# Expert weights of a mixture layer moved as one transfer per expert on one Trainium2 core

## The reference, cut to what matters

```python
combine = jnp.sum(jax.nn.one_hot(expert_idx, N_EXPERTS, dtype=jnp.float32) * weights[..., None], axis=1)
for e in range(N_EXPERTS):
    h = jax.nn.silu(t @ w_gate[e]) * (t @ w_up[e])
    out = out + combine[:, e:e + 1] * (h @ w_down[e])
```

## Time and profile before

| | |
|---|---|
| Median of 3 runs | 1083.51 us (1080.67 to 1083.88) |
| The profiled execution, its time | 1081.82 us |
| Its span, from the first to the last instruction | 1080.1 us |
| Busy share of the span: PE matmul, PE weight load | 76%, 59% |
| Busy share: DVE, ACT, POOL | 29%, 18%, 1% |
| Mean granted PE clock, as a share of 2.4 GHz | 0.902 |
| Read from HBM, mean rate | 437.84 MB, 406 GB/s |
| Chain that ended last, by engine | DMA 61%, PE 34%, ACT 2% |
| Weight transfers of experts (gate, up, down into the ring) | 62, 62, 60 of 2048 KB |

### The profile page before, as it was taken

One profiled execution on the slowest core, in us unless ns is written; L12 is line 12 of the kernel. 1 busy time (PEld: TensorE's weight loads), 2 busy tenths in 40 slices (PEclk: granted clock), 3 DMA queues, 4 the chain that ended last, 5 costly groups with the idle time before them and its releaser, 6 DMA issues.

```text
span 1080.1 us, 30413 instructions
## 1 busy us (share of the span) xinstructions
PE 817.0 (76%) x13908; PEld 634.1 (59%) x13909; DVE 315.9 (29%) x783; ACT 193.4 (18%) x358; POOL 5.5 (1%) x26
## 2 busy tenths in 40 slices
PE   7999997665666767586799998967576766766864
PEld 7888665554454545464499986745354554544652
DVE  5764522111111111121277744311111111111212
ACT  6674211000000000010163330100000000000002
POOL 1000000000000000000000000000000000000000
PEclk9999899888898888988999999988889888798988
DMA  9977999999999999999998599999999999999996
GB/s 356 426 296 313 408 427 429 430 428 428 428 428 429 428 429 430 428 427 424 418 427 361 220 396 420 428 428 429 429 427 428 429 428 428 428 431 428 425 424 255
DMA packets 35872, 439.62 MB, mean 407 GB/s; under 512 B 4208, under 2 KB 4976, under 8 KB 9968
## 3 DMA queue, kind: packets, MB, share of 16 engines
q1 hardware_dynamic: 34848, 437.58, 96.3%
q10 hardware_dynamic: 976, 1.33, 0.4%
HBM read 437.84 MB, written 1.05 MB: 406 GB/s over the span
## 4 chain that ended last, share of the span: by engine, by line
DMA 61%; PE 34%; ACT 2%; issue 2%; DVE 1%; SPq 0%; ACTq 0%; DVEq 0%
DMA ring<-in_w_up 34%; DMA ring<-in_w_down 27%; PE psum L1295 8%; PE psum L1487 8%; PE psum L1360 4%; PE psum L1496 4%; PE psum L1504 2%; PE psum L1342 2%; PE psum L1516 2%; PE psum L1274 1%; PE psum L1568 1%; DMA ring<-in_even_first 1%; PE psum L1510 1%; ACT ring_halves L538 0%; PE psum L1267 0%
## 5 line engine op out<-in xcount | busy, mean ns | idle before, releaser
L1487 PE MATMUL psum<-ring,m 128*32 128x128 f32 x7936 | 309.7, 321 | 220.8 <-DMA ring<-in_w_gate 106.7
L1487 PEld LDWEIGHTS psum<-ring,m 128*32 128x32 f32 x7936 | 271.8, 130 | 266.2 <-issue 114.3
L1160 DVE TENSOR_TENSOR m<-psum,m 128x128 f32<-128x128 f32 x64 | 18.7, 292 | 568.5 <-ACT m L703 568.5
L1496 PE MATMUL psum<-ring,m 128*32 128x256 f32 x1984 | 121.1, 382 | 15.6 <-DMA ring<-in_w_down 11.5
L703 ACT ACTIVATE m<-psum 128x128 f32<-128x128 f32 x64 | 17.7, 277 | 519.1 <-PE psum L1487 519.1
L1295 PE MATMUL psum<-scr_halves,ring_halves 128*128 128x256 f32 x768 | 105.2, 284 | 5.1 <-DVE ring_halves L802 4.5
L1496 PEld LDWEIGHTS psum<-ring,m 128*32 128x32 f32 x1984 | 65.8, 111 | 64.3 <-issue 22.6
L1295 PEld LDWEIGHTS psum<-scr_halves,ring_halves 128*128 128x128 f32 x768 | 99.3, 192 | 5.7 <-DVE ring_halves L802 4.9
L1504 PE MATMUL psum<-m 32*128 32x256 f32 x1056 | 84.8, 427 | 8.0 <-issue 5.9
L802 DVE TENSOR_TENSOR ring_halves<-ring,ring_halves 128x2048 fp32r<-128x2048 f32 (+2 forms) x37 | 68.6, 1885 | 13.6 <-ACT ring_halves L538 13.5
L1516 PE MATMUL psum<-x,m 128*32 128x256 f32 x1024 | 71.1, 397 | 0.0
(11 more groups left out here) (192 smaller groups left out, 483.9 us busy)
## 6 DMA issues: line engine op xcount, KB each, us to landing
ring<-in_w_gate SPq DMA_DIRECT2D x62, 2048.0 KB, 40.5
ring<-in_w_up SPq DMA_DIRECT2D x62, 2048.0 KB, 40.6
ring<-in_w_down SPq DMA_DIRECT2D x60, 2048.0 KB, 41.1
ring<-in_odd_w_in SPq DMA_DIRECT2D x5, 2048.0 KB, 26.1
ring<-in_even_w_in SPq DMA_DIRECT2D x3, 2048.0 KB, 20.6
ring<-in_even_w_out SPq DMA_DIRECT2D x2, 2048.0 KB, 30.4
spare<-in_w_down SPq DMA_DIRECT2D x2, 2048.0 KB, 22.9
ring<-in_last_down SPq DMA_DIRECT2D x8, 512.0 KB, 36.7
```

Of the source, the lines that this page charges most:

```text
L1487: last = pe.matmul(GU[CAP * part:CAP * (part + 1), lo:lo + FP], block_of(k), w_of(k)[:, FP * part:FP * (part + 1)], start=k == 0, stop=k = ...
L1496: last = pe.matmul(YB[CAP * part:CAP * (part + 1), 0:DP], hhT[:, CAP * f:CAP * (f + 1)], w[:, f, DP * part:DP * (part + 1)], start=f == 0, ...
```

## The change

The weights of an expert are laid out by the host as one array, in which each partition's row holds gate, up and down behind each other (48 KB). What follows from that in the kernel:

- Experts 6 to 30 are loaded **whole**: one transfer of 128 rows of 48 KB into three slots side by side, after a wait for `y_ready` of the expert three before. Experts 0, 1, 3, 4, 5 and 31 keep single transfers of one matrix (16 KB rows), as does expert 2.
- EARLY is **expert 2** instead of 27: it lies in the mixers' buffers, and experts 0, 1 and 3 (RING_FIRST) are those that are in the ring first. The order of the first loads in layer 1 begins with the down matrix of expert 3.
- Slots are numbered from another start (`place`), and one entry of the ring (HOLE) is left empty between the odd mixer and layer 1, so that three slots of an expert lie side by side.
- The overflow part moves to the **middle** of the layer (after expert 14) on every engine, SP's part between the loads of expert 17 and 18. It uses another of the three token buffers.
- The loops: PE has experts 0 to 5 written out, then a loop of three experts for 6 to 14, the overflow part, a second loop of three for 15 to 29, and experts 30 and 31 written out. That is 14 bodies of `expert` per layer. DVE and ACT have two loops of three, and two written out.

```diff
-EARLY = TURNS * TRI
-DRAIN = EARLY + 1
+EARLY = 2
+RING_FIRST = (0, 1, 3)
+MIDDLE = 5
+PAUSE = MIDDLE * TRI - 1
+SPARE_XG = 1
...
+FINE = 2 * TRI
+ROLLED = FINE // TRI
...
+def is_whole(e):
+    return FINE <= e < NE - 1
...
             def first(l, i, mat):
-                n = L_MOE[l] + 3 * i + mat
-                fill(n, matrix(l, i, mat), buffer(n, mat))
-
-            def expert(l, b, i):
-                e = b * TRI + i
-                for mat, used in enumerate((gate_used, gu_ready, y_ready)):
-                    n = L_MOE[l] + 3 * i + mat
-                    sp.wait_ge(used, after(l, e - TRI))
-                    load(n, matrix(l, e, mat), buffer(n, mat))
...
+                n = entry(l, RING_FIRST[i]) + mat
+                fill(n, matrix(l, RING_FIRST[i], mat), buffer(n, mat))
+
+            def second(l, e):
+
+                for mat in range(3):
+                    n = entry(l, e) + mat
+                    fill(n, matrix(l, e, mat), buffer(n, mat))
+
+            def whole(l, e, i, former):
+
+                sp.wait_ge(y_ready, after(l, former))
+                at = third(l, (i - 1) % TRI) * 3 * SLOT
+                sp.dma_start(ring[:, at:at + 3 * SLOT], expert_weights_in[l, e]).then_inc(whole_landed[third(l, (i - 1) % TRI)], 16)
...
+                for e in range(EARLY + 2, FINE):
+                    second(l, e)
+                for i in range(TRI):
+                    e = FINE + i
+                    whole(l, e, i, e - TRI)
+                turns(l, ROLLED + 1, MIDDLE + 1)
+                overflow(l)
+                turns(l, MIDDLE + 1, TURNS)
...
-                with pe.Fori(0, TURNS) as T:
-                    for i in range(TRI):
-                        expert(l, T, i)
-                for e in range(EARLY, NE):
-                    expert(l, e // TRI, e % TRI, rest=True)
-                    if e == DRAIN:
-                        scatter_result(l, e)
+                for e in range(FINE):
+                    expert(l, e // TRI, e % TRI)
+                for start, stop in ((ROLLED, MIDDLE), (MIDDLE, TURNS)):
+                    with pe.Fori(start, stop) as T:
+                        for i in range(TRI):
+                            expert(l, T, i)
+                    if start == ROLLED:
                         more_experts(l)
+                for e in range(TURNS * TRI, NE):
+                    expert(l, e // TRI, e % TRI)
```

More of the change, by code:

```diff
@@ L38 @@
 TRI = 3
[L39 to L40 removed]
+TURNS = NE // TRI
 MAX_MORE = (S - 1) // CAP
@@ L59, with entry, place, third @@
 SPLIT = [L_EVEN + i for i in range(7)] + [L_ODD + i for i in range(8)]
+def entry(l, e):
+    return L_MOE[l] + 3 * (e - (e > EARLY))
+def place(n):
+    return (n + 2) % RING
+def third(l, i):
+    return place(L_MOE[l] + 3 * i) // 3
+def is_whole(e):
+    return FINE <= e < NE - 1
+SINGLE = [z for z in SPLIT if z not in (L_EVEN, L_EVEN + 1, L_ODD)]
+for layer in range(2):
+    for expert in range(FINE):
+        if expert != EARLY:
+            SINGLE += [entry(layer, expert) + mat for mat in range(3)]
+    SINGLE += [entry(layer, NE - 1) + mat for mat in range(2)]
+SINGLE.append(L_GAIN)
+WHOLE = [(layer, expert) for layer in range(2) for expert in range(NE) if is_whole(expert)]
+def single_count(n):
+    return sum(z <= n and place(z) == place(n) for z in SINGLE)
+def whole_count(l, e):
+    return sum((zl, ze) <= (l, e) and place(entry(zl, ze)) == place(entry(l, e)) for zl, ze in WHOLE)
 def pieces(n):
@@ L198, in trunk @@
         landed = [sem(f"landed{i}") for i in range(RING)]
+        whole_landed = [sem(f"whole_landed{i}") for i in range(RING // 3)]
         gate_used, out_half = sem("gate_used"), sem("out_half")
@@ L291, in is_split, with wait_landed @@
         def is_split(n):
[L292 to L297, removed]
+            return n in SPLIT
+        def wait_landed(eng, n):
+            eng.wait_ge(landed[place(n)], 16 * single_count(n))
         @contextmanager
@@ L417, in experts, with turns, overflow @@
+            def turns(l, start, stop):
+                with sp.Fori(start, stop) as b:
+                    for i in range(TRI):
+                        whole(l, b * TRI + i, i, b * TRI + (i - TRI))
+            def overflow(l):
                 X = xs[l]
@@ L420, in experts @@
                     with each() as (e, r, n):
-                        for mat, w in enumerate((w_gate, w_up, w_down)):
+                        for mat in range(3):
                             sp.wait_ge(X[("done", "gate", "gu")[mat]], n)
+                            src = matrix(l, e, mat)
                             if mat < 2:
-                                src = w[l, e].rearrange("(p k) f -> p k f", k=K)
                                 dst = xb.rearrange("p (k f) -> p k f", k=K)
                             else:
-                                src = w[l, e].rearrange("(p j) d -> p j d", p=P)
                                 dst = xb.rearrange("p (j d) -> p j d", j=4)
                             sp.dma_start(dst, src).then_inc(X["landed"], 16)
+            def experts(l):
+                if l:
+                    first(l, 2, 2)
+                    load_spare(l)
+                first(l, 0, 0)
+                first(l, 0, 1)
+                if l == 0:
+                    load_spare(l)
+                first(l, 0, 2)
+                first(l, 1, 0)
+                if l == 0:
+                    first(l, 1, 1)
+                sp.wait_ge(*((even_lo, 6), (pb_ready, 4))[l])
+                load_early(l, 0, 0, 1)
+                first(l, 1, 2 - l)
+                first(l, 2, 1 - l)
+                load_early(l, 1, 0, 2)
+                first(l, 1 + (l == 0), 2 * l)
+                first(l, 2, 2 - l)
+                load_early(l, 1, 1, 2)
+                for e in range(EARLY + 2, FINE):
[6 more added lines that the diff above has]
+                turns(l, MIDDLE + 1, TURNS)
+                for e in range(TURNS * TRI, NE - 1):
+                    whole(l, e, e % TRI, e - TRI)
+                n = entry(l, NE - 1)
+                for mat in range(2):
+                    fill(n + mat, matrix(l, NE - 1, mat), buffer(n + mat, mat))
+                sp.wait_ge(*used_up(n + 2 - RING))
+                for j in range(NP):
+                    sp.dma_start(tall(n + 2)[:, j, :], last_down[l, j]).then_inc(quarter_landed[j], 16)
             for i, ks in enumerate(PIECES):
@@ L720, in moe @@
                 preload(ACT.Silu)
-                with act.Fori(0, TURNS) as b:
-                    for i in range(TRI):
[L723 to L727, removed]
+                for start, stop in ((0, MIDDLE), (MIDDLE, TURNS)):
+                    with act.Fori(start, stop) as b:
+                        for i in range(TRI):
+                            expert(l, b * TRI + i)
+                    if start == 0:
+                        more_experts(l)
+                for e in range(TURNS * TRI, NE):
                     expert(l, e)
@@ L1188, in moe @@
                 more_blocks(l)
-                with dve.Fori(0, TURNS) as b:
-                    for i in range(TRI):
-                        expert(l, b, i)
+                for start, stop in ((0, MIDDLE), (MIDDLE, TURNS)):
+                    with dve.Fori(start, stop) as b:
+                        for i in range(TRI):
+                            expert(l, b, i)
+                    if start == 0:
+                        more_experts(l)
                 for e in range(TURNS * TRI, NE):
@@ L1523, in scatter_result, with expert, wait_weights @@
                 return scatter()
-            def expert(l, T, i, rest=False):
+            def expert(l, T, i):
                 e = T * TRI + i
-                n, turns = (rest_entry(l, e), 0) if rest else (L_MOE[l] + 3 * i, T)
+                known = isinstance(e, int)
                 block_of = lambda k: xg[:, i, k, :]
+                if known:
+                    n = entry(l, e)
+                else:
+                    n = entry(l, ROLLED * TRI + i)
+                def wait_weights(mat):
+                    if known and not is_whole(e):
+                        wait_landed(pe, n + mat)
+                    elif mat == 0:
+                        turn = e // TRI - ROLLED if known else T + (-ROLLED)
+                        pe.wait_ge(whole_landed[place(n) // 3], (turn + whole_count(l, ROLLED * TRI + i)) * 16)
                 pe.wait_ge(xg_ready, after(l, e))
                 for mat, used in enumerate((gate_used, gu_ready)):
-                    if rest and e == EARLY:
+                    if known and e == EARLY:
                         pe.wait_ge(early_landed[mat], (32, 64)[mat] * (l + 1))
```

103 lines of the change are left out of this document (35 added, 68 removed).

## The result

The changed kernel takes 1092.39 us (median of 6 runs, 1088.34 to 1094.96) against 1083.97 us for the kernel before on the same chip (6 runs). The ratio is 1.0081, with a 95% interval of 1.0065 to 1.0097: slower by 0.8%. Run again later beside other kernels, it took 1092.46 us against 1081.34, ratio 1.0099 (1.0081 to 1.0118). By the intervals of the ratios, each such effect is known to 2 to 3 us.

A forecast was written before the change was run, and what follows sets the result against it. It took the kernel to be bound by DMA weight transfers, 14.68 us per expert, with PE waiting. Terms -5.5 + 12.7 + 2.3 + 3.0 = +12.5 us on 1081.8 gave 1094.3, or 1096.0 us as median; range 1085 to 1110.

The forecast's parts named there:

- Part 1: Whole-expert loads: one transfer of 48 KB rows saves 0.11 us per expert, -5.5 us over 25 experts in each layer.
- the line: Row cost in full DMA queues: 6.7 ns per row plus 37.8 ns per KB, giving 1821 ns for 48 KB.
- The rival in which the row is cut anyway: Whole-expert loads: rows are cut into 16 KB pieces, so the long row gains nothing; 1102 us, chance 0.12.
- the case for 14.40 us: Whole-expert loads: 432 GB/s throughout and no fixed row cost, gaining 14.0 us; used in a rival at 1077.9 us, chance 0.10.
- The fixed cost of 2.0 us: Every transfer: if each paid this beside its bytes, two fewer in 50 experts would save 200 us; given no chance.
- Part 2: After expert 5's load in each layer: DMA runs dry until PE finishes expert 3; holes of 7.4 and 5.3 us, +12.7 us.
- Part 3: PE's code: 14 bodies per layer instead of eight, nineteen more code packets through the DMA engines, +2.3 us.
- Part 4: End of each layer: PE begins whole expert 30 later and stops for code at expert 31; 1.5 us per layer, +3.0 us.
- Part 5: Mid-layer overflow part and whole experts' waits for `y_ready`: both covered by queued loads, costing nothing.

The follow-up runs named there:

- the first edit: Changed kernel with expert 5 instead of 2 in the mixers' buffers and experts 0, 1, 2 first in the ring: 1083.36 us, ratio 1.0011 to the kernel before.
- the one with experts 6 to 8: Changed kernel with experts 6, 7 and 8 also loaded as single matrices and written out on PE: 1085.98 us, ratio 1.0041 to the kernel before.
- One loop: Changed kernel with a single loop for experts 6 to 29 on PE, ACT and DVE, overflow part left out: 1090.06 us, ratio 1.0069 to the kernel before.
- the edit of expert 30: Changed kernel with expert 30 loaded as three single matrices again: 1087.68 us, ratio 1.0038 to the kernel before.

## Why the prediction was right

It gave 1096.0 us, a range of 1085 to 1110 and slower with 0.85. It came out slower, 12.5 us forecast and 8.4 or 11.1 measured against the kernel before. By its own steps:

- **Part 1, the long row: -5.5 us forecast, -7.3 measured.** Landings are 14.53 us apart, not 14.57: a row of 48 KB costs 1817 ns where the line gave 1821. Cutting the rows gave back 7.3 us, and 50 times 0.15 is 7.5. The rival in which the row is cut anyway is out, and so is the case for 14.40 us. The fixed cost of 2.0 us, which the prediction set aside, stands in the Trainium skill (DMA: Bandwidth & Descriptors, section "Anatomy of one DMA") for transfers that POOL starts. SP starts these, so the trace does not test it; no term rests on it.
- **Part 2, the hole: +12.7 us forecast; 9.2 and 13.2 in the two profiles, 10.8 to 13.6 in the three others that kept it, 8.5 by the first edit.** The mechanism is as described: both the place of expert 2 and the wait for all three slots are needed, as the first edit and the one with experts 6 to 8 show. The edit gave back less than the holes, as its own landings behind that point are 1.5 us late in each layer. Two sizes were off, and that they cancelled in part is luck. The restart of an empty queue costs 18.2 - 14.5 = 3.7 us for a whole expert, not 2.6. And in the first profile the load of expert 6, which waits for expert 3, was started only 1.0 and 0.5 us after the queue was dry, against 4.8 and 2.7 forecast. The second profile has 5.4 us in layer 0, and in layer 1 the load was started 0.2 us before.
- **Part 3, the code: +2.3 us forecast.** Nineteen more packets came, as counted. One loop takes away 13 of them. It is faster by 2.3 us, which is within noise, and some 2.7 us of late landings go. By the landings that is 0.2 us a packet where the forecast had 0.12, so nineteen would cost about 4 us (an estimate), inside the bounds.
- **Part 4, the tail: +3.0 us forecast, 5.6 measured** by the edit of expert 30. This is the step whose reason failed. It expected PE to stand for code at expert 31. PE did not; it lost the time on expert 30 itself, at the lower clock level after its wait, so that in layer 1 the up step of expert 31 began 13.7 us after the start of expert 30 and not 11.0 or a little more. From the profiles: 3.0 and 3.6 us later against the last landing in the first, and 1.5 and 2.4 in the second. Some 1.4 us have to be taken off in layer 0, where the last expert's gate weights now land 4.9 us after expert 30 instead of 6.3. That is 5.2 and 2.5 us in sum; the forecast lies between.
- **Part 5, nothing for the overflow part and the waits:** right for the waits, since whole experts land 14.53 us apart. That the place of the overflow part is worth 10 us at the other end was not seen.

The measured terms add up: -7.3 + 8.5 + 2.3 + 5.6 = 9.1 us, where the two comparisons have 9.7 in the mean. Each is known to 2 to 3 us only, so that they meet this closely is in part luck. Against the forecast they are off by -1.8, -4.2, 0.0 and +2.6 us, so its total was nearer than its parts. That the change was slower although the rate rose is settled by runs: without the two losses it is faster than the kernel before. What sets the size of the hole from run to run is open.

## What to carry to other kernels

A longer transfer is gained byte by byte, but it is paid where the stream begins and ends: it can start only when all of its room is free, and it can be used only when all of it is there. So keep the first and the last of a series in pieces, and give buffers that free no room to one that comes after the stream is running. Where an engine's program is long, count its written-out code as traffic, and keep jumps over unused code away from the stretch in which that engine sets the end.

## What was not expected of the hardware

- A transfer of 6 MB into an empty queue needed 3.7 to 4.0 us more than in a full one (18.2 and 18.5 us against 14.5); for 2 MB it was 2.6 us (7.5 against 4.9).
- After a wait of 5.2 us PE's next 128 matmuls ran at a granted clock of 0.53 and took 6.43 us instead of 3.68; after one of 5.1 us in the second profile it was 0.73 and 4.99 us. In the middle of the stream such matmuls cost nothing (the landings stay 14.53 us apart); at its end they were 1.3 to 2.8 us.
- A jump over a part of the program that isn't run stopped PE for 5.7 to 7.4 us beside full DMA queues, about as long as a packet of code took to follow another there (6.2 to 7.2 us).
